# Seven of 22 gate and up tile pairs of a feed-forward block by Strassen's identity instead of five, with the input sums made earlier and laid partly into the weight slots

## The chip, the cores and the metric

One core of one Trainium2 chip runs the kernel. The metric is the device time of one execution in microseconds (us). The kernel before takes 2000.92 us (median of three runs, 2000.67 to 2001.42).

## What is computed

The reference is a model of two layers on 512 tokens of width 1024 with 16 meta tokens in front, so 528 token columns. A layer is a feed-forward block, a mixer (a gated linear recurrence beside a latent attention) and a second feed-forward block. All is float32. The change touches the feed-forward blocks alone:

```python
D_MODEL = 1024
D_FF = 11 * D_MODEL // 4

def swiglu(u, w_gate, w_up, w_down):
    return (jax.nn.silu(u @ w_gate) * (u @ w_up)) @ w_down

for l in range(DEPTH):
    f = swiglu(rms_norm(h, ffn1_pre_g[l]), ffn1_w_gate[l], ffn1_w_up[l], ffn1_w_down[l])
    h = h + 0.5 * rms_norm(f, ffn1_post_g[l])
    ...
    h = h + rms_norm(y, mix_post_g[l])
    f = swiglu(rms_norm(h, ffn2_pre_g[l]), ffn2_w_gate[l], ffn2_w_up[l], ffn2_w_down[l])
    h = h + 0.5 * rms_norm(f, ffn2_post_g[l])
return h[:, N_META:]
```

## The kernel before, in words

**Layout and precision.** Features lie on the 128 partitions, tokens along the free dimension. The tokens are split into two halves of 264 columns. The last feed-forward block needs only the 512 real tokens, so its halves have 256 columns. A float32 product is made of three matmuls: high part of the weights by high part of the input, high by low, low by high. The input's parts are `xh` and `xl`, the weights' are `whi` and `wlo`.

**Blocks.** Six blocks run one after another (b = 0 to 5); blocks 0, 2, 3 and 5 are feed-forward blocks, 1 and 4 are mixers. A feed-forward block has 22 pairs of a gate tile and an up tile (m = 0 to 21), each tile with 8 chunks of 128 input features, and then the down product from `hidh` and `hidl`, the two parts of the hidden values. The first three tiles are interleaved in `opening` (L1871), because their input arrives half by half; all later ones go through `product` (L1821) or `strassen` (L1833).

**Weight slots.** Every weight tile takes the next of four slots in turn. SyncE loads it into `raw` (`load`, L663), ScalarE rounds it into `whi` (`hi`, L789), and GpSimd subtracts the two into `wlo` in four pieces (`lo`, L741) or VectorE does in one (`low`, L1464). TensorE waits for that low part at the head of each tile (`slot_in`, L1815). A slot has 11 x 128 columns, since a down tile needs them; a gate or up tile uses 8 x 128. Tile numbers count from the block's first: in a plain pair m they are 2m and 2m + 1 as long as no Strassen pair came before.

**Strassen pairs.** A pair m in `STRASSEN` (L119: 5, 7, 9, 11, 13) does gate and up together as a 2 x 2 block product with seven half products instead of eight: rows are the gate's and the up's weights, the inner split is between the upper and the lower four feature chunks, columns are the two token halves. Such a pair takes four slots, of the kinds gate, s13, s2up and s4. The kinds s13 and s4 are sums of weights that VectorE makes in `raw` (`sums`, L1439), and VectorE makes their low parts too. The seven half products are 12 matmuls of half a token row each:

```python
part(n[1], False, sums(0), bank(uu, trim, 1))
pe.wait_ge(part_copied, q + 1)
part(n[1], True, sums(2), bank(z, trim, 0)).then_inc(slots_used, 1)
```

The first half product stands in PSUM until ScalarE copies it out (`part_copy`, L992), and the fourth half product reuses its bank, which is the wait in the middle line. VectorE joins the seven results in `strassen_sums` (L1471).

**Input sums.** The sums of input chunks are the same for every Strassen pair of a block and are made once, in four steps k = 0 to 3. Step k: ScalarE writes the scaled chunks k and k + 4 into `t_in` (`sum_inputs`, L977); VectorE makes four sums of them in `t_sum`, each of half a token row (`t_sums`, L1420, the instructions of L1428 to L1431); ScalarE rounds them into `t_hi` (`sum_hi`, L987); VectorE subtracts into `t_lo` (`t_low`, L1433). There is one `t_in` and one `t_sum`, so a step's sums wait for the step before. TensorE waits for all four steps once per block, before its first s13 tile.

**Order.** Each engine works through a list written out by hand. ScalarE's loop over m (L1001) is: silu, the rounding of the tiles 2m + 4 and 2m + 5, and the rounding of the hidden values (`hid_hi`, L974), with the parts of the input sums between them. VectorE's loop (L1500) is: gate out of PSUM (L1395), up out of PSUM (L1403), their product `hid` (L1411), its low part (`hid_lo`, L1416), and between them `sums`, `low`, `t_low` and `t_sums`. The silu waits for gate, hid for silu, hid_hi for hid, and hid_lo for hid_hi, so ScalarE and VectorE wait for each other twice in every pair. TensorE has four pairs of PSUM banks in turn; before the last chunk of a tile it waits until the next tile's banks have been read (`unit_free`, L1818).

Of the kernel before, what the change touches and what calls it, by code (L numbers as in the profile page):

```python
# [25 lines left out]
F32 = mybir.dt.float32  # L26
F32R = mybir.dt.float32r
BF16 = mybir.dt.bfloat16
ALU = mybir.AluOpType
ACT = mybir.ActivationFunctionType  # L30
AX = mybir.AxisListType

P = 128
# [4 lines left out]
T = N_META + SEQ  # L38
HALF = T // 2
D = 1024  # L40
DC = D // P
# [12 lines left out]
RING = 4  # L54
# [61 lines left out]
DVE_TAIL = (0, 2, 4, 6, 7)  # L116


STRASSEN = (5, 7, 9, 11, 13)  # L119
KH = DC // 2  # L120
T_SUMS = 4


def build_program(nc, a, out, depth, d_ff):
    FC = d_ff // P
    FH = FC // 2
    MAXT = max(FH, DC)
# [1 line left out]
    assert FC % 2 == 0 and FC >= 6  # L129


    assert FC - DC > max(STRASSEN) and FC - DC - 4 > min(STRASSEN) > 4


    tiles = []
# [2 lines left out]
    for b in range(NB):  # L138
# [4 lines left out]
        for m in range(FC):  # L143
            n = len(tiles)
# [17 lines left out]
    for n in range(NSLOT):  # L162
        made[n in LO_DVE] += 1
        LO_N[n] = made[n in LO_DVE]
        if KIND.get(n) not in ("s13", "s4"):
# [5 lines left out]
                     k=4, q=HEADS, statl=1, v=len(V_UNITS), tr=WC, out=DC)  # L171
    U = {}
    n = 0
# [10 lines left out]
    for b in range(NB):  # L184
        if b % 3 != 1:
            n = U[b, "gu"]
# [100 lines left out]
    with ExitStack() as ctx:  # L287
# [4 lines left out]
        base = [(nc.sbuf_base + 31) // 32 * 32]  # L292

        def sb_at(name, offset, shape, dt):
            return nc.alloc_sbuf_tensor_at(name, shape, dt, offset=offset)

        def sb(name, shape, dt):
            size = 2 if dt == BF16 else 4
            for s in shape[1:]:
                size *= s  # L300
            t = sb_at(name, base[0], shape, dt)
            base[0] += (size + 31) // 32 * 32
            return t

        CH = T * 4
# [4 lines left out]
        xl = sb("xl", [P, DC, T], F32R)  # L310
        tail_step = sb_at("tail_step", xh_at, [P, DC, T], F32)
        f_ffn = sb_at("f_ffn", xl_at, [P, DC, T], F32)
        raw = sb("raw", [P, RING, MAXT * P], F32)
        whi = sb("whi", [P, RING, MAXT * P], F32R)
        wlo = sb("wlo", [P, RING, MAXT * P], F32R)
# [10 lines left out]
        arena = base[0]  # L326
# [1 line left out]
        hidh = sb_at("hidh", arena, [P, FC, T], F32R)  # L328
        hidl = sb_at("hidl", arena + FC * CH, [P, FC, T], F32R)

        t_hi = sb_at("t_hi", arena + (FC - DC) * CH, [P, KH, T_SUMS, HALF], F32R)
        t_lo = sb_at("t_lo", arena + (2 * FC - DC) * CH, [P, KH, T_SUMS, HALF], F32R)
        t_in = sb_at("t_in", arena + (FC - DC - 4) * CH, [P, 2, T], F32)
        t_sum = sb_at("t_sum", arena + (FC - DC - 2) * CH, [P, T_SUMS, HALF], F32)

        off = [arena]

# [162 lines left out]
        t_hi_ready = sem("t_hi_ready")  # L500
# [279 lines left out]
        def _(act):  # L780
# [8 lines left out]
            def hi(n):  # L789
                if n < NSLOT:  # L790
                    r, k = n % RING, tiles[n] * P

                    if n in PREV:
                        act.wait_ge(slots_used, slot_used(PREV[n]))
                    if KIND.get(n) in ("s13", "s2up", "s4"):
                        act.wait_ge(w_sums, 3 * STRASSEN_N[n] + ("s13", "s2up", "s4").index(KIND[n]) + 1)
                    else:
                        act.wait_ge(raw_full[r], 16 * LOADED_N[n])
                    nc.scalar.activation(w_hi(n)[:, 0:k], raw[:, r, 0:k], ACT.Copy).then_inc(hi_ready, 1)  # L799
# [160 lines left out]
            def ffn(b):  # L960
                s0, f0 = slot0[b], (b // 3 * 2 + b % 3 // 2) * FC
                u0, trim = U[b, "gu"], b > 0 and trimmed(b - 1)

                F = b // 3 * 2 + b % 3 // 2
                g = ("ffn1_pre_g", "mix_pre_g", "ffn2_pre_g")[b % 3]

                def silu(m):
                    ug = GATE_U[b, m]
                    act.wait_ge(psum_free[pair_of(ug)], read_out(ug))
                    nc.scalar.activation(toks(tmp[2], trim), toks(tmp[0], trim), ACT.Silu).then_inc(silu_ready, 1)  # L970

                def hid_hi(m):
                    act.wait_ge(hid_ready, f0 + m + 1)
                    nc.scalar.activation(toks(hidh[:, m, :], trim), toks(tmp[3], trim),  # L974
                                         ACT.Copy).then_inc(hidh_ready, 1)

                def sum_inputs(k):  # L977

                    if k:
                        act.wait_ge(t_sum_ready, KH * F + k)  # L980
                    for i in range(2):
                        c = k + i * KH
                        ins = nc.scalar.activation(toks(t_in[:, i, :], trim), toks(h[:, c, :], trim), ACT.Copy,
                                                   scale=col(g, b // 3, c))
                    ins.then_inc(t_in_ready, 1)

                def sum_hi(k):  # L987
                    act.wait_ge(t_sum_ready, KH * F + k + 1)
                    nt = span(trim, 0)[1]
                    nc.scalar.activation(t_hi[:, k, :, 0:nt], t_sum[:, :, 0:nt], ACT.Copy).then_inc(t_hi_ready, 1)  # L990

                def part_copy(m):  # L992

                    q = STRASSEN_N[TILES_OF[b, m][0]]
                    act.wait_ge(part_mm, 2 * q + 1)
                    if q:
                        act.wait_ge(part_added, 6 * q)
                    nc.scalar.activation(half(tmp[4], trim, 0), bank(FIRST_U[b, m], trim, 0), ACT.Copy)\
                        .then_inc(part_copied, 1)

                for m in range(FC):  # L1001
                    n = TILES_OF[b, m]
                    if m in STRASSEN:
                        part_copy(m)
                        for i in range(3):
                            hi(n[i] + RING)
                        silu(m)
                        hi(n[3] + RING)
                        hid_hi(m)
                        continue  # L1010
                    silu(m)
                    if m:
                        hi(n[0] + RING)
                    if m == 1:
                        sum_hi(0)
                        sum_inputs(1)
                    hid_hi(m)
                    hi(n[1] + RING)
                    if 0 < m < 4:
                        sum_hi(m)  # L1020
                    if m < 3 and m != 1:
                        sum_inputs(0 if m == 0 else 3)
                    elif m == 1:
                        sum_inputs(2)
                tables(LN_EXP_TABLES)
                for m in range(DC - split[b]):
                    hi(out_slot(b, m) - 1 + RING)
                    output_chunk(b, m)
                    hi(out_slot(b, m) + RING)
# [194 lines left out]
        def _(dve):  # L1224
# [158 lines left out]
            def ffn(b):  # L1383
# [36 lines left out]
                def t_sums(k):  # L1420
# [9 lines left out]
                    chain.link(nc.vector.tensor_tensor(t2, b22, t1, ALU.subtract))  # L1430
                    nc.vector.tensor_tensor(t4, b21, t2, ALU.subtract).then_inc(t_sum_ready, 1)  # L1431

                def t_low(k):  # L1433
                    dve.wait_ge(t_hi_ready, KH * F + k + 1)
                    nt = span(trim, 0)[1]
                    nc.vector.tensor_tensor(t_lo[:, k, :, 0:nt], t_sum[:, :, 0:nt],
                                            t_hi[:, k, :, 0:nt].bitcast(F32), ALU.subtract).then_inc(t_lo_ready, 1)

                def sums(n):  # L1439

# [60 lines left out]
                for m in range(FC):  # L1501
                    n = TILES_OF[b, m]
                    nxt = [i + RING for i in n]
                    sums(nxt[0])
                    if m in STRASSEN:
                        strassen_sums(m, 0)
                        sums(nxt[1])
                        low(nxt[0])
                        sums(nxt[2])
                        low(nxt[1])  # L1510
                        strassen_sums(m, 1)
                        strassen_sums(m, 2)
                        low(nxt[2])
                        strassen_sums(m, 3)
                        gate(m)
                        up(m)
                        sums(nxt[3])
                        hid(m)
                        low(nxt[3])
                        hid_lo(m)  # L1520
                        continue
                    gate(m)
                    if m == 1:
                        t_sums(0)
                    elif 2 <= m <= 4:
                        t_low(m - 1)
                    sums(nxt[1])
                    low(nxt[0])
                    up(m)
                    hid(m)  # L1530
                    low(nxt[1])
                    hid_lo(m)
                    if m == 1:
                        t_low(0)
                    if 1 <= m <= 3:
                        t_sums(m)
                    if b == 0 and m == FC - 4:
                        decay_rates()
                output_sum(b)
# [251 lines left out]
        def _(pe):  # L1791
# [41 lines left out]
            def strassen(b, m, trim, following):  # L1833
# [18 lines left out]
                    return lambda k: (xh[:, k + upper * KH, at:at + nt], xl[:, k + upper * KH, at:at + nt])  # L1852

                def sums(i):
                    return lambda k: (t_hi[:, k, i, 0:nt], t_lo[:, k, i, 0:nt])

                slot_in(n[0])
                part(n[0], False, tokens(0, a0), bank(z, trim, 0), ug).then_inc(part_mm, 1)
# [473 lines left out]
```

## Time and profile before

| | |
|---|---|
| median of three runs | 2000.92 us (2000.67 to 2001.42) |
| the profiled execution | 2001.3 us, of which the span from first to last instruction is 1999.5 us |
| TensorE matmul busy | 1986.0 us, 99% of the span, 15084 instructions |
| VectorE, ScalarE, GpSimd busy | 913.9, 824.6, 1029.3 us |
| DMA | 175.76 MB, mean 88 GB/s |
| mean granted clock | 0.999 |

Busy times overlap one another. A busy TensorE says nothing of how well it is fed; what matters is where its stream of matmuls breaks. A matmul's own duration is longer than its share of the stream, since they are pipelined, so lengths of work on TensorE are read as differences of start times.

### The profile page before, as it was taken

The numbers are of one execution on the slowest core, as the hardware profiler recorded it, in microseconds if no ns is written. First come the engines' busy times: TensorE is split into PE (matmuls) and PEld (weight loads), VectorE is DVE, ScalarE is ACT, GpSimd is POOL, SyncE is SP. The second block draws the span as 40 slices with busy tenths as digits, with TensorE's granted clock in tenths as the row PEclk, the third lists the DMA queues.
The fourth block names the chain that finished last, engine by engine and source line by source line (L and its number), as shares of the span: only waits on it lengthen the run. The fifth ranks groups of instructions, "written<-read, shape, count | busy, mean of one in ns | idle before, by whom it ended". The sixth has DMA issues, their size and how long they took to land.

```text
span 1999.5 us, 35699 instructions
## 1 busy us (share of the span) xinstructions
PE 1986.0 (99%) x15084; PEld 1909.5 (96%) x15084; DVE 913.9 (46%) x1433; ACT 824.6 (41%) x1318; POOL 1029.3 (51%) x1257
## 2 busy tenths in 40 slices
PE   9999999999999999999999999999999999999998
PEld 9999999999899999999999999999998998888887
DVE  6663310478546765210076542103785467642102
ACT  6433222465555533232264332224555465332321
POOL 3655554576315655454375554544763256564551
PEclk9999999999999999999999999999999999999999
DMA  4224332132201223332122333321322112333321
GB/s 167 86 94 125 103 102 86 67 96 80 64 33 43 85 85 127 100 117 88 57 75 85 96 117 111 102 84 62 101 82 65 33 54 74 109 124 107 116 73 43
DMA packets 48479, 175.76 MB, mean 88 GB/s; under 512 B 5184, under 2 KB 9408, under 8 KB 48320
## 3 DMA queue, kind: packets, MB, share of 16 engines
q1 hardware_dynamic: 48176, 173.40, 26.6%
q8 instruction: 118, 1.93, 0.4%
q14 instruction: 41, 0.34, 0.1%
q10 hardware_dynamic: 144, 0.10, 0.0%
HBM read 171.38 MB, written 2.10 MB: 87 GB/s over the span
## 4 chain that ended last, share of the span: by engine, by line
PE 98%; DVE 1%; ACT 1%; DMA 0%; issue 0%; SPq 0%; DVEq 0%
PE ps L1803 97%; PE ps L2184 1%; DMA h<-in_x 0%; DVE osb L1751 0%; ACT xh L829 0%; DVE xl L1761 0%; DVE tail_step L1295 0%; PE ps L2063 0%; DVE probT L1719 0%; ACT prob L1151 0%; DVE small L1728 0%; DVE h L1300 0%; ACT tmp L1187 0%; ACT xh L1202 0%; DVE wlo L1329 0%
## 5 line engine op out<-in xcount | busy, mean ns | idle before, releaser
L747 POOL TENSOR_TENSOR wlo<-raw,whi 128x256 fp32r<-128x256 f32 (+2 forms) x1148 | 944.0, 854 | 726.2 <-ACT whi L799 723.6
L1803 PE MATMUL ps<-xh,whi 128*128 128x264 f32 (+2 forms) x2680 | 645.3, 296 | 3.2 <-DVE xl L1334 1.5
L1803 PE MATMUL ps<-xl,whi 128*128 128x264 f32 (+2 forms) x2680 | 641.7, 295 | 0.0
L1803 PE MATMUL ps<-xh,wlo 128*128 128x264 f32 (+2 forms) x2680 | 640.8, 295 | 0.0
L1803 PEld LDWEIGHTS ps<-xh,whi 128*128 128x128 f32 x2680 | 445.0, 188 | 17.4 <-DVE wlo L1329 2.3
L799 ACT ACTIVATE whi<-raw 128x1024 fp32r<-128x1024 f32 (+3 forms) x329 | 356.0, 1083 | 255.7 <-PE ps L1803 221.6
L1803 PEld LDWEIGHTS ps<-xl,whi 128*128 128x128 f32 x2680 | 443.7, 188 | 11.4
L1803 PEld LDWEIGHTS ps<-xh,wlo 128*128 128x128 f32 x2680 | 443.6, 189 | 10.5
L1803 PE MATMUL ps<-hidh,whi 128*128 128x264 f32 (+2 forms) x1276 | 313.6, 296 | 0.0
L1803 PE MATMUL ps<-hidl,whi 128*128 128x264 f32 (+2 forms) x1276 | 312.5, 295 | 0.0
L1803 PE MATMUL ps<-hidh,wlo 128*128 128x264 f32 (+2 forms) x1276 | 312.4, 295 | 0.0
L1373 DVE TENSOR_TENSOR tmp<-tmp,tmp 128x264 f32<-128x264 f32 (+3 forms) x52 | 36.2, 696 | 414.5 <-ACT tmp L862 361.1
L1803 PEld LDWEIGHTS ps<-hidl,whi 128*128 128x128 f32 x1276 | 214.4, 188 | 6.2
L1803 PEld LDWEIGHTS ps<-hidh,wlo 128*128 128x128 f32 x1276 | 214.0, 188 | 5.9
L1803 PEld LDWEIGHTS ps<-hidh,whi 128*128 128x128 f32 x1276 | 213.3, 188 | 6.0
L1403 DVE TENSOR_TENSOR tmp<-ps,rs_in 128x528 f32<-128x528 f32 (+1 forms) x88 | 61.6, 700 | 211.7 <-PE ps L1803 211.7
L974 ACT ACTIVATE hidh<-tmp 128x528 fp32r<-128x528 f32 (+1 forms) x88 | 56.2, 639 | 233.3 <-DVE tmp L1411 233.3
L970 ACT ACTIVATE tmp<-tmp 128x528 f32<-128x528 f32 (+1 forms) x88 | 56.4, 641 | 182.9 <-DVE tmp L1395 182.4
L1395 DVE TENSOR_TENSOR tmp<-ps,rs_in 128x528 f32<-128x528 f32 (+1 forms) x88 | 61.7, 701 | 98.0 <-PE ps L1803 82.3
L763 POOL TENSOR_TENSOR tmp<-tmp,tmp 128x264 f32<-128x264 f32 (+1 forms) x55 | 45.7, 830 | 103.3 <-ACT tmp L836 100.5
L1803 PE MATMUL ps<-t_lo,whi 128*128 128x264 f32 (+1 forms) x320 | 90.5, 283 | 0.0
L1803 PE MATMUL ps<-t_hi,whi 128*128 128x264 f32 (+1 forms) x320 | 90.5, 283 | 0.0
(218 smaller groups left out, 2332.8 us busy)
## 6 DMA issues: line engine op xcount, KB each, us to landing
raw<-in_ffn_up SPq DMA_DIRECT2D x88, 512.0 KB, 3.7
raw<-in_ffn_down SPq DMA_DIRECT2D x64, 704.0 KB, 4.0
raw<-in_ffn_gate SPq DMA_DIRECT2D x87, 512.0 KB, 3.6
raw<-in_w_in SPq DMA_DIRECT2D x28, 512.0 KB, 3.5
raw<-in_w_out SPq DMA_DIRECT2D x16, 512.0 KB, 3.6
raw<-in_w_q SPq DMA_DIRECT2D x8, 384.0 KB, 3.2
out_t<-h SPq DMA_DIRECT2D x16, 128.0 KB, 1.8
h<-in_x SPq DMA_DIRECT2D x2, 528.0 KB, 5.7
```

What stands on the lines that cost most here:

```text
L747: ins = nc.gpsimd.tensor_tensor(w_lo(n)[:, at], raw[:, r, at], w_hi(n)[:, at].bitcast(F32), ALU.subtract)
L763: nc.gpsimd.tensor_tensor(hs, hs, square_of(k, s, trim), ALU.add)\
L799: nc.scalar.activation(w_hi(n)[:, 0:k], raw[:, r, 0:k], ACT.Copy).then_inc(hi_ready, 1)
L970: nc.scalar.activation(toks(tmp[2], trim), toks(tmp[0], trim), ACT.Silu).then_inc(silu_ready, 1)
L974: nc.scalar.activation(toks(hidh[:, m, :], trim), toks(tmp[3], trim), ACT.Copy).then_inc(hidh_ready, 1)
L1373: nc.vector.tensor_tensor(acc, acc, part(tmp[m % 2], trim), ALU.add).then_inc(sum_ready, 1)
L1395: nc.vector.tensor_tensor(halves(tmp[0], trim), unit(ug, trim, trim and m > 1 and m not in STRASSEN), halves(rs_in, trim), ALU.mult).then_ ...
L1403: nc.vector.tensor_tensor(halves(tmp[1], trim), unit(uu, trim, trim and m > 0 and m not in STRASSEN), halves(rs_in, trim), ALU.mult).then_ ...
L1803: return nc.tensor.matmul(o, w, x, start=start, stop=stop)
L2184: ins = nc.tensor.transpose(ps[:, c0:c0 + P], prob[e % 4][:, k0:k0 + P], ident)
```

## The change

The pairs that use the identity become 4, 6, 8, 10, 12, 14 and 16. The four steps of input sums no longer have a place of their own behind the hidden values: step 0's parts lie in columns 1024 to 1287 of the slots of `whi` and `wlo`, step 1's high part in the same columns of `raw` and its low part in the last hidden chunk, steps 2 and 3 in hidden chunks 17 to 20. The steps are placed earlier in both engines' lists: ScalarE copies step 0's input ahead of the first silu, and VectorE makes step 0's sums at the end of pair 0, step 1's and 2's in pair 1, step 3's at the end of pair 2.

```diff
-STRASSEN = (5, 7, 9, 11, 13)
+STRASSEN = (4, 6, 8, 10, 12, 14, 16)
...
-        t_hi = sb_at("t_hi", arena + (FC - DC) * CH, [P, KH, T_SUMS, HALF], F32R)
-        t_lo = sb_at("t_lo", arena + (2 * FC - DC) * CH, [P, KH, T_SUMS, HALF], F32R)
-        t_in = sb_at("t_in", arena + (FC - DC - 4) * CH, [P, 2, T], F32)
-        t_sum = sb_at("t_sum", arena + (FC - DC - 2) * CH, [P, T_SUMS, HALF], F32)
+        hid_all = sb_at("hid_all", arena, [P, 2, FC, T], F32R)
+        raw_spare = sb_at("raw_spare", raw_at, [P, RING, MAXT * P], F32R)
+        spare = slice(DC * P, DC * P + HALF)
+
+        def four(first, which):
+            return hid_all[:, which, first:first + 2, :].rearrange("p a (i t) -> p (a i) t", i=2)
+
+        last = hid_all[:, :, FC - 1, :].rearrange("p a (i t) -> p a i t", i=2)
+        T_HI = [whi[:, :, spare], raw_spare[:, :, spare], four(FC - 5, 0), four(FC - 3, 0)]
+        T_LO = [wlo[:, :, spare], last, four(FC - 5, 1), four(FC - 3, 1)]
...
+        t_in = sb_at("t_in", arena + (FC - 9) * CH, [P, 2, T], F32)
+        t_sum = sb_at("t_sum", arena + (FC - 7) * CH, [P, T_SUMS, HALF], F32)
...
+                sum_inputs(0)
                 for m in range(FC):
...
                     if m == 1:
+                        sum_hi(1)
+                        sum_inputs(2)
+                    hid_hi(m)
+                    hi(n[1] + RING)
+                    if m == 0:
                         sum_hi(0)
                         sum_inputs(1)
-                    hid_hi(m)
-                    hi(n[1] + RING)
-                    if 0 < m < 4:
-                        sum_hi(m)
-                    if m < 3 and m != 1:
-                        sum_inputs(0 if m == 0 else 3)
                     elif m == 1:
-                        sum_inputs(2)
+                        sum_hi(2)
+                        sum_inputs(3)
+                    elif m == 2:
+                        sum_hi(3)
...
                     gate(m)
                     if m == 1:
-                        t_sums(0)
-                    elif 2 <= m <= 4:
-                        t_low(m - 1)
+                        t_low(0)
+                        t_sums(1)
+                    elif 2 <= m <= 3:
+                        t_low(m)
                     sums(nxt[1])
                     low(nxt[0])
                     up(m)
                     hid(m)
                     low(nxt[1])
                     hid_lo(m)
-                    if m == 1:
-                        t_low(0)
-                    if 1 <= m <= 3:
-                        t_sums(m)
+                    if m == 0:
+                        t_sums(0)
+                    elif m == 1:
+                        t_low(1)
+                        t_sums(2)
+                    elif m == 2:
+                        t_sums(3)
...
                 def sums(i):
-                    return lambda k: (t_hi[:, k, i, 0:nt], t_lo[:, k, i, 0:nt])
+                    return lambda k: (t_one(T_HI, k, i, nt), t_one(T_LO, k, i, nt))
```

## Rows read from the trace of the kernel before

**Rows 1.** The page's first part, busy time of each engine.
```profile
PE 1986.0 (99%) x15084; PEld 1909.5 (96%) x15084; DVE 913.9 (46%) x1433; ACT 824.6 (41%) x1318; POOL 1029.3 (51%) x1257
```

**Rows 2.** Waits of TensorE: who for whom, total, times, longest (us).
```profile
PE ps L1803 <- DVE xl L1334: 1.5, 2, 1.0
```

**Rows 3.** Timeline of TensorE, blocks 0 and 5: start, duration, instruction.
```profile
57.75 0.41 PE L1803 MATMUL ps<-xh,whi 128*128 128x264 f32 x2
...
69.49 0.28 PE L1803 MATMUL ps<-xh,whi 128*128 128x264 f32 x1
...
73.89 0.28 PE L1803 MATMUL ps<-t_hi,whi 128*128 128x264 f32 x1
...
79.71 0.40 PE L1803 MATMUL ps<-xh,whi 128*128 128x264 f32 x2
...
1672.11 0.40 PE L1803 MATMUL ps<-xh,whi 128*128 128x512 f32 x1
...
1683.23 0.28 PE L1803 MATMUL ps<-xh,whi 128*128 128x256 f32 x1
...
1687.48 0.28 PE L1803 MATMUL ps<-t_hi,whi 128*128 128x256 f32 x1
...
1693.10 0.39 PE L1803 MATMUL ps<-xh,whi 128*128 128x512 f32 x1
```

**Rows 4.** Timeline of ScalarE, the first pairs of block 0.
```profile
29.93 0.65 ACT L970 ACTIVATE tmp<-tmp 128x528 f32<-128x528 f32 x1
...
32.91 1.35 ACT L983 ACTIVATE t_in<-h,par 128x528 f32<-128x528 f32 x2
...
37.51 1.09 ACT L990 ACTIVATE t_hi<-t_sum 128x1056 fp32r<-128x1056 f32 x1 [1.76 <-DVE t_sum L1431]
```

**Rows 5.** Timeline of VectorE, the first five pairs of block 0.
```profile
32.09 0.71 DVE L1416 TENSOR_TENSOR hidl<-tmp,hidh 128x528 fp32r<-128x528 f32 x1 [0.71 <-ACT hidh L974]
...
34.30 0.52 DVE L1428 TENSOR_TENSOR t_sum<-t_in 128x264 f32<-128x264 f32 x1 [0.88 <-ACT t_in L983]
...
40.42 0.71 DVE L1416 TENSOR_TENSOR hidl<-tmp,hidh 128x528 fp32r<-128x528 f32 x1 [1.08 <-ACT hidh L974]
...
42.40 0.78 DVE L1428 TENSOR_TENSOR t_sum<-t_in 128x264 f32<-128x264 f32 x1
...
45.77 0.69 DVE L1395 TENSOR_TENSOR tmp<-ps,rs_in 128x528 f32<-128x528 f32 x1
47.00 1.26 DVE L1436 TENSOR_TENSOR t_lo<-t_sum,t_hi 128x1056 fp32r<-128x1056 f32 x1 [0.54 <-ACT t_hi L990]
...
59.47 1.21 DVE L1411 TENSOR_TENSOR tmp<-tmp,tmp 128x528 f32<-128x528 f32 x1
...
64.10 0.43 DVE L1428 TENSOR_TENSOR t_sum<-t_in 128x264 f32<-128x264 f32 x1
...
65.73 0.68 DVE L1455 TENSOR_TENSOR raw<-raw 128x512 f32<-128x512 f32 x1
66.33 0.70 DVE L1395 TENSOR_TENSOR tmp<-ps,rs_in 128x528 f32<-128x528 f32 x1
66.96 1.26 DVE L1436 TENSOR_TENSOR t_lo<-t_sum,t_hi 128x1056 fp32r<-128x1056 f32 x1
```

**Rows 6.** Timeline of GpSimd, block 0: two tiles' low parts.
```profile
33.09 6.86 POOL L747 TENSOR_TENSOR wlo<-raw,whi 128x256 fp32r<-128x256 f32 x8 [2.61 <-ACT whi L799]
```

**Rows 7.** The page's sixth part: loads of up tiles, KB each, us to landing.
```profile
raw<-in_ffn_up SPq DMA_DIRECT2D x88, 512.0 KB, 3.7
```

**Rows 8.** Timelines of VectorE and ScalarE, pair 4 of block 5.
```profile
1681.80 0.69 DVE L1395 TENSOR_TENSOR tmp<-ps,rs_in 128x512 f32<-128x512 f32 x1
...
1686.66 0.36 ACT L998 ACTIVATE tmp<-ps 128x256 f32<-128x256 f32 x1
```

**Rows 9.** Windows, end of the run: length, busy by engine, granted clock, DMA.
```profile
1992.00:1994.00 2.00, 0.00 (x0) 0.00 (x0) 1.31 (x4) 0.63 (x2) 0.48 (x1) 1.00 0.00 0
...
1996.00:1999.50 3.50, 0.00 (x0) 0.00 (x0) 1.11 (x4) 0.00 (x0) 0.36 (x1) 0.50 0.59 198
```

More of the change, by code:

```diff
@@ L129, in build_program @@
     assert FC % 2 == 0 and FC >= 6
-    assert FC - DC > max(STRASSEN) and FC - DC - 4 > min(STRASSEN) > 4
+    assert FC - 5 > max(STRASSEN) and FC - 9 > min(STRASSEN) > 3 and FH >= DC + 3
     tiles = []
@@ L312, in build_program @@
         f_ffn = sb_at("f_ffn", xl_at, [P, DC, T], F32)
+        raw_at = base[0]
         raw = sb("raw", [P, RING, MAXT * P], F32)
@@ L329, in build_program, with t_half, t_one, t_whole @@
         hidl = sb_at("hidl", arena + FC * CH, [P, FC, T], F32R)
-        t_hi = sb_at("t_hi", arena + (FC - DC) * CH, [P, KH, T_SUMS, HALF], F32R)
-        t_lo = sb_at("t_lo", arena + (2 * FC - DC) * CH, [P, KH, T_SUMS, HALF], F32R)
-        t_in = sb_at("t_in", arena + (FC - DC - 4) * CH, [P, 2, T], F32)
-        t_sum = sb_at("t_sum", arena + (FC - DC - 2) * CH, [P, T_SUMS, HALF], F32)
+        hid_all = sb_at("hid_all", arena, [P, 2, FC, T], F32R)
[6 more added lines that the diff above has]
+        T_LO = [wlo[:, :, spare], last, four(FC - 5, 1), four(FC - 3, 1)]
+        def t_half(part, k, nt):
+            at = part[k]
+            if at is last:
+                return at[:, :, :, 0:nt]
+            return at[:, :, 0:nt]
+        def t_one(part, k, i, nt):
+            at = part[k]
+            if at is last:
+                return at[:, i // 2, i % 2, 0:nt]
+            return at[:, i, 0:nt]
+        def t_whole(k, nt):
+            at = t_sum[:, :, 0:nt]
+            return at.rearrange("p (a i) t -> p a i t", i=2) if T_LO[k] is last else at
+        t_in = sb_at("t_in", arena + (FC - 9) * CH, [P, 2, T], F32)
+        t_sum = sb_at("t_sum", arena + (FC - 7) * CH, [P, T_SUMS, HALF], F32)
         off = [arena]
@@ L1431, in t_sums, with t_high @@
                     nc.vector.tensor_tensor(t4, b21, t2, ALU.subtract).then_inc(t_sum_ready, 1)
+                def t_high(k, nt):
+                    at = t_half(T_HI, k, nt).bitcast(F32)
+                    return at.rearrange("p (a i) t -> p a i t", i=2) if T_LO[k] is last else at
                 def t_low(k):
@@ L1435, in t_low @@
                     nt = span(trim, 0)[1]
-                    nc.vector.tensor_tensor(t_lo[:, k, :, 0:nt], t_sum[:, :, 0:nt],
-                                            t_hi[:, k, :, 0:nt].bitcast(F32), ALU.subtract).then_inc(t_lo_ready, 1)
+                    nc.vector.tensor_tensor(t_half(T_LO, k, nt), t_whole(k, nt), t_high(k, nt), ALU.subtract).then_inc(t_lo_ready, 1)
                 def sums(n):
```

2 lines of the change are left out of this document (1 added, 1 removed).

## Prediction, made before the changed kernel was run

> **What bounds the kernel now.** The page's busy times come first: TensorE's matmuls fill 1986.0 of 1999.5 us and no other engine is over 52% [rows 1]. Then the waits of TensorE: its longest kind of wait in the matmul line totals 1.5 us [rows 2]. So time is the number of matmuls times their spacing, as long as nothing starves the stream; an engine at half load costs nothing unless it is late at one place. The timeline of TensorE gives the spacing [rows 3]: plain pair 4 of block 0 runs from 57.75 to 69.49, 11.74 us for 96 matmuls of 264 columns, and Strassen pair 5 from 69.49 to 79.71, 10.22 us for 84. Both come to 0.122 us per matmul, so that weights used once instead of twice in a row cost nothing. In block 5 a plain pair (48 matmuls of 512 columns) takes 1683.23 - 1672.11 = 11.12 us and a Strassen pair (84 of 256) 1693.10 - 1683.23 = 9.87 us. The remaining question is whether the first Strassen pair, now pair 4, finds its operands in time; for that I read ScalarE, VectorE and GpSimd at the block's start.
>
> **The gain.** Each of the four blocks gets two more Strassen pairs. In blocks 0, 2 and 3: 6 x (11.74 - 10.22) = 9.1 us. In block 5: 2 x (11.12 - 9.87) = 2.5 us. Together 11.6 us, all on TensorE's path. The Trainium skill (TensorE: Matmul & The Clock Gate, "Wait — 56ns, not 53.3ns?") puts the spacing of back-to-back matmuls at N / 2.4 GHz plus about 2.5 ns, 112.5 ns for 264 columns; the trace has 122, and by the page six pairs would save 8.1 us instead of 9.1.
>
> **What the new pairs ask of the others.** A Strassen pair adds weight sums, PSUM sums and the low parts of s13 and s4 on VectorE, one rounding more on ScalarE, nothing on GpSimd (it makes two low parts per pair in both kinds) and no bytes (two loads either way). The Strassen and plain pairs alternate as before, and between pairs 5 and 14 TensorE shows no wait of weight [rows 2], so I cost pairs 6 to 16 at nothing beyond their matmuls. Their cover is the plain pair in between. The decay work of block 0 at m = 18 stays behind a plain pair.
>
> **The first Strassen pair comes 11.7 us sooner, its input sums do not.** TensorE starts the fourth half product of the pair, the one behind the part copy, 73.89 - 69.49 = 4.40 us after the pair's start [rows 3]. With pair 4 this place moves to 57.75 + 4.40 = 62.15 us in block 0. Against it stands a chain of ScalarE and VectorE that does not depend on TensorE, since all tiles it needs are long done. I follow it from rows of the old order, step by step; starts of consecutive instructions on one engine lie about 0.1 us closer than their durations.
>
> 1. ScalarE copies step 0's input ahead of silu(0): 1.35 us [rows 4], so silu(0) starts at 31.2 instead of 29.93. The low part of hidden chunk 0, at 32.09 before [rows 5], starts at 33.35, and VectorE is free for the first sums at 34.0.
> 2. Sums of step 0. Before, they took from 34.30 to the rounding at 37.51, 3.2 us [rows 4, 5], while GpSimd worked [rows 6]; the same sums with GpSimd idle take 65.73 - 64.10 = 1.6 us [rows 5]. The two slow each other. Tile 5's rounding is 1.3 us later too, so GpSimd runs from about 34.3 to 37.8 (6.86 us for two tiles [rows 6]): I take the slow price, and the rounding starts at 37.2.
> 3. Rounding of step 0 and input of step 1 (1.09 and 1.35 us [rows 4]): 39.6.
> 4. Sums of step 1. GpSimd's next tile waits for silu(1) and a rounding behind that input, about 41.1, so the fast price holds: 41.3.
> 5. Rounding of step 1, input of step 2, rounding of hidden chunk 1. The old distance from a rounding at 37.51 to the low part at 40.42 held the same three: 2.9 us [rows 4, 5], giving 44.25. Then the low parts of chunk 1 and of step 1, as from 40.42 to 42.40, 2.0 us: 46.25.
> 6. Sums of step 2 with GpSimd on tile 7: 42.40 to 45.77, 3.4 us [rows 5]; gate(2) starts at 49.6. Low part of step 2 done 47.00 + 1.26 - 45.77 = 2.5 us later: 52.1.
> 7. Two s13 weight sums at 0.68 us [rows 5] and up(2), 0.6: hid(2) starts at 54.0. The load of tile 10 that they need is issued when tile 6's low part is done, about 44.5, and lands after 3.7 us [rows 7], 4 us ahead.
> 8. From hid(2) over the rounding and low part of s13 to the sums of step 3: 64.10 - 59.47 = 4.6 us [rows 5], 58.65. From there to gate(3): 66.33 - 64.10 = 2.2 us, 60.9.
> 9. From gate(3) to the end of t_low(3): 66.96 + 1.26 - 66.33 = 1.9 us, 62.8. From gate(3) to the end of the part copy, which stands in ScalarE's list behind silu(3), tile 10, hid_hi(3) and tile 11: 1686.66 + 0.36 - 1681.80 = 5.2 us where up did not wait [rows 8], plus up to 0.5 us if hid(3) meets GpSimd (1.21 us, against 0.71 for a low part of the same size [rows 5]): 66.4.
>
> So TensorE, which wants the third half product at 62.15 - 12 x 0.122 = 60.7, waits about 2.1 us for the last low part, then computes 1.5 us, then waits about 2.1 us for the part copy: 4.25 us in all. In the kernel before the same t_low was done at 68.2 against a need at 72.4: four us of slack, and the chain has gained only 5.4 us (gate at 66.33 before, 60.9 now) where TensorE's need has moved by 11.74.
>
> In block 5 the old gate(4) started 1687.48 - 1681.80 = 5.7 us ahead of the fourth half product [rows 3, 8], in block 0 73.89 - 66.33 = 7.6 us. Moving need by 11.12 and gate by 5.4 leaves no lead at all, so the wait is the 5.45 us of step 9. Blocks 2 and 3 I take like block 0, having the same forms. Sum: 3 x 4.25 + 5.45 = 18.2 us of waits. What is queued behind: VectorE and ScalarE don't wait on TensorE here, but SyncE's loads of tiles 12 and 13 wait for the last weight sum of pair 4; they land before TensorE is through with the delayed pair.
>
> The new places of the sums (spare columns of slots, other hidden chunks) have the same sizes and partitions; I cost them at nothing, from below and above by at most 2% of a 1.26 us subtraction.
>
> **Sum.** -11.6 + 18.2 = +6.6 us. The profiled execution took 2001.3 us, 0.4 above the median, so it would be 2007.9, and the median 2007.5.
>
> **Bounds.** What the rows don't settle is whether GpSimd is in its pieces at each sum. Down: step 0's sums at the fast price, -1.6, both hid products fast, -0.75: a wait of 1.9 in the first three and 3.1 in block 5 leaves 1998.1. Up: step 1's sums slow as well, +1.7, and hid(3) slow, +0.25: 6.2 and 7.4 us, 2015.3. I take middle values as the order of starts says; not all ends come at once.
>
> **Rivals.**
> *The chain arrives in time.* If it were under 2.9 us late on average (11.6 / 4), the change gains. That needs 1.4 us less than my steps in every block, for instance step 0's sums ahead of GpSimd. For it: the wide gap between the two prices, and that the slow one depends on a few tenths. Against: steps 3, 5, 8 and 9 are plain latencies between two engines that repeat within 0.1 us. With no wait at all the time is 1989.3; with half of it, 1998.4.
> *More contention.* A later tile 5 on GpSimd overlaps step 1's sums and passes the delay on: up to 7 us more, 2014.
> *The clock falls during the waits.* Granted clock stayed at 1.00 (2.4 GHz) in a 2 us window without a single matmul and showed 0.50 (1.2 GHz) only in the last window, over 5 us after the last matmul [rows 9]. My waits are two pieces near 2 us with 12 matmuls in between, so I expect no fall. If the remaining 48 matmuls of pair 4 ran at the lower level, each block would lose 48 x 0.122 = 5.9 us, 2031. The Trainium skill (TensorE: Matmul & The Clock Gate, "What's actually happening") says that the throttled state is the default and activity releases it; by that rule a fall is possible, and the rows speak against it here.
> *The change doesn't shorten the pairs*, because matmuls reading sums beside weights in one slot are slower: the gain is gone, the wait stays, 2019. No row shows such a conflict.
>
> **How the numbers follow.** About 0.2%, 4 us, is what a measurement of this kernel can tell from no change. Forecast, with waits of 3.1 to 6.2 us per block on average, 2001 to 2014: 0.78; of it 0.10 lies under 2004.9, where the waits average under 3.9 us against my 4.55. In time or half so, clearly faster: 0.10. Between the two, 1997 to 2001: 0.03. Contention beyond the range 0.04, the clock 0.03, no saving 0.02, all slower. So faster 0.10, same 0.10 + 0.03 = 0.13, slower 0.68 + 0.09 = 0.77. The range is the forecast's own, 2001 to 2014; it holds the bounds above but for the corner where every doubt falls one way, and leaves out the in-time case, the clock and the lost saving.
>
> **What would show it.** Right: in each feed-forward block the waits of TensorE name t_lo (or gate(3)'s read) and the part copy, some 4 to 5.5 us together; pairs of 10.2 and 11.7 us alternate from pair 6 on; gate(3) at 60.9 and the part copy ending at 66.4 in block 0; granted clock 1.00. Wrong: no wait in pair 4 (then time near 1989), waits in pair 6 or later, or a matmul spacing off 0.122 us.

## The result and the profile after

The changed kernel takes 2012.12 us (median of five runs, 2010.93 to 2012.76) against 2000.8 us before (median of five runs), a ratio of 1.0056 with a 95% interval of 1.0041 to 1.0070: 11.3 us slower. The forecast was 2007.5 us, slower, in a range of 2001 to 2014. The profiled execution is the slowest of the five, so what is read from its trace adds up to 0.6 us more than the median.

| | before | after |
|---|---|---|
| profiled execution, span | 2001.3 us, 1999.5 us | 2012.76 us, 2011.0 us |
| matmul busy | 1986.0 us | 1982.4 us |
| mean granted clock | 0.999 | 0.994 |

The waits of TensorE come first (who for whom, total, times, longest; the matmul helper is now L1840). Before, the longest kind of wait in this line totalled 1.5 us [rows 2]:

```profile
PE ps L1840 <- ACT tmp L1025: 6.8, 4, 2.2
PE ps L1840 <- DVE tmp L1425: 5.4, 4, 1.7
PE ps L1840 <- DVE hid_all L1470: 2.4, 4, 0.7
...
PE ps L1840 <- POOL wlo L774: 0.4, 1, 0.4
```

Three waits occur four times, once per feed-forward block: for the part copy (L1025), for the read of gate(3) (L1425), and for the last low part of the input sums (L1470). The forecast named all three, the first two of them as one piece. The timeline of TensorE shows them inside pair 4 of block 0:

```profile
57.49 0.29 PE L1840 MATMUL ps<-xh,whi 128*128 128x264 f32 x1
...
61.45 0.40 PE L1840 MATMUL ps<-xh,whi 128*128 128x264 f32 x1 [1.25 <-DVE tmp L1425]
...
62.73 0.36 PE L1840 MATMUL ps<-whi 128*128 128x264 f32 x1 [0.63 <-DVE hid_all L1470]
...
64.02 0.64 PE L1840 MATMUL ps<-hid_all,whi 128*128 128x264 f32 x2
64.46 0.42 PE L1840 MATMUL ps<-hid_all,wlo 128*128 128x264 f32 x1
66.61 0.59 PE L1840 MATMUL ps<-whi 128*128 128x264 f32 x1 [1.73 <-ACT tmp L1025]
...
74.29 0.41 PE L1840 MATMUL ps<-xh,whi 128*128 128x264 f32 x2
```

The pair runs from 57.49 to 74.29, 16.8 us instead of the 10.2 of an undisturbed one. And a matmul of 264 columns at 66.61 has a duration of 0.59 us, where the same form has 0.28 elsewhere: the clock. Windows of 3 us over that stretch (length; busy of TensorE, its weight loads, VectorE, ScalarE, GpSimd; granted clock; DMA):

```profile
60.00:63.00 3.00, 1.11 (x7) 0.73 (x6) 3.00 (x5) 2.66 (x3) 0.00 (x0) 1.00 0.00 0
63.00:66.00 3.00, 1.88 (x12) 1.57 (x10) 2.05 (x3) 0.90 (x3) 2.90 (x4) 0.62 0.58 164
66.00:69.00 3.00, 2.38 (x11) 2.39 (x12) 1.66 (x3) 1.62 (x3) 1.09 (x3) 0.50 0.93 343
69.00:72.00 3.00, 3.00 (x21) 3.00 (x21) 0.34 (x1) 1.06 (x1) 3.00 (x5) 0.74 0.07 23
```

After a window with 7 matmuls the granted clock falls to 0.50, the lower level of 1.2 GHz, and comes back inside the window from 69 to 72. It fell before the wait for the part copy began: from 64.02 to 64.46 two matmuls start 0.22 us apart instead of 0.12, and that wait begins only behind them. In blocks 3 and 5, where the clock fell too, it was the same. The next two windows lie there, ahead of the wait for the part copy; the two waits before it were 1.23 and 0.65 us in block 3, 1.73 and 0.51 in block 5:

```profile
1070.70:1071.40 0.70, 0.70 (x5) 0.61 (x3) 0.70 (x1) 0.00 (x0) 0.70 (x2) 0.50 0.30 70
...
1685.10:1686.00 0.90, 0.39 (x3) 0.12 (x2) 0.90 (x2) 0.90 (x2) 0.00 (x0) 0.50 0.00 0
```

In block 2 the same waits left it at 1.00:

```profile
684.00:687.00 3.00, 1.50 (x10) 1.33 (x11) 3.00 (x5) 2.28 (x3) 0.51 (x1) 1.00 0.00 0
687.00:690.00 3.00, 0.82 (x7) 0.61 (x6) 1.74 (x3) 1.44 (x3) 2.76 (x4) 1.00 0.76 231
```

The chain of VectorE and ScalarE, by the rows of the same instructions as in the forecast:

```profile
49.53 0.69 DVE L1425 TENSOR_TENSOR tmp<-ps,rs_in 128x528 f32<-128x528 f32 x1
...
53.88 0.97 DVE L1441 TENSOR_TENSOR tmp<-tmp,tmp 128x528 f32<-128x528 f32 x1
...
58.47 0.42 DVE L1458 TENSOR_TENSOR t_sum<-t_in 128x264 f32<-128x264 f32 x1
...
60.69 0.70 DVE L1425 TENSOR_TENSOR tmp<-ps,rs_in 128x528 f32<-128x528 f32 x1
61.32 1.26 DVE L1470 TENSOR_TENSOR hid_all<-t_sum,hid_all 128x1056 fp32r<-128x1056 f32 x1
```

```profile
36.95 1.09 ACT L1017 ACTIVATE whi<-t_sum 128x1056 fp32r<-128x1056 f32 x1 [2.92 <-DVE t_sum L1461]
...
66.19 0.37 ACT L1025 ACTIVATE tmp<-ps 128x264 f32<-128x264 f32 x1
```

Rounding of step 0 at 36.95 (forecast 37.2), gate(2) at 49.53 (49.6), hid(2) at 53.88 (54.0), the sums of step 3 at 58.47 (58.65), gate(3) at 60.69 (60.9), t_low(3) done at 62.6 (62.8), the part copy done at 66.56 (66.4). The whole block begins 0.24 us earlier in this execution. With that taken off, gate(3) and t_low(3) came as worked out within 0.05 us, and the part copy 0.4 us later: the steps from gate(3) to its end were that much longer.

**Where the 11.6 us went.** From the last matmul of one pair to the last of the next, in the changed kernel pair 4 takes 16.80, 15.06, 16.83 and 16.06 us in blocks 0, 2, 3 and 5, where undisturbed Strassen pairs of the same trace take 10.19 and, in block 5, 10.06. That is 24.1 us too much. With pair 4 counted at its undisturbed length, all pairs together are 12.5 us shorter than before. In every pair from 5 on there is no wait. 24.1 - 12.5 = 11.6 us, which is the whole difference of the two spans within 0.1.

### The profile page after: what moved, and what is told of

Read it like the earlier page. It is cut to its first block, busy times and chain, and to the rows that moved or that the text cites. A ratio compares the mean times of both kernels' runs of the same rounds, so it can differ in the third digit from the quotient of the medians.

```text
span 2011.0 us, 35915 instructions
## 1 busy us (share of the span) xinstructions
PE 1982.4 (99%) x15084; PEld 1906.8 (95%) x15084; DVE 967.1 (48%) x1537; ACT 841.4 (42%) x1342; POOL 1023.8 (51%) x1257
## 4 chain that ended last, share of the span: by engine, by line
PE 90%; DVE 5%; ACT 3%; issue 1%; DMA 0%; DVEq 0%; SPq 0%; ACTq 0%
PE ps L1840 89%; PE ps L2221 1%; DVE tmp L1441 1%; DVE t_sum L1459 1%; DVE t_sum L1461 1%; DVE t_sum L1460 0%; ACT t_in L1010 0%; DVE t_sum L1458 0%; ACT whi L826 0%; DVE hidl L1446 0%; DVE tmp L1433 0%; ACT hidh L1001 0%; ACT L813 0%; DVE wlo L1470 0%; DMA h<-in_x 0%
## 5 line engine op out<-in xcount | busy, mean ns | idle before, releaser
L1840 PE MATMUL ps<-xh,whi 128*128 128x264 f32 (+2 forms) x2552 | 621.1, 296 | 9.0 <-DVE tmp L1425 5.4
L1840 PE MATMUL ps<-xl,whi 128*128 128x264 f32 (+2 forms) x2552 | 616.0, 294 | 0.0
L1840 PE MATMUL ps<-xh,wlo 128*128 128x264 f32 (+2 forms) x2552 | 615.6, 294 | 0.0
L826 ACT ACTIVATE whi<-raw 128x1024 fp32r<-128x1024 f32 (+3 forms) x345 | 369.8, 1073 | 298.8 <-PE ps L1840 250.4
L1840 PEld LDWEIGHTS ps<-xh,whi 128*128 128x128 f32 x2552 | 426.7, 188 | 22.9 <-DVE tmp L1425 6.3
L1840 PEld LDWEIGHTS ps<-xl,whi 128*128 128x128 f32 x2552 | 425.5, 188 | 10.0
L1840 PEld LDWEIGHTS ps<-xh,wlo 128*128 128x128 f32 x2552 | 425.3, 188 | 9.1
L1840 PE MATMUL ps<-hidh,whi 128*128 128x264 f32 (+2 forms) x1276 | 313.5, 296 | 0.0
L1840 PE MATMUL ps<-hidl,whi 128*128 128x264 f32 (+2 forms) x1276 | 312.3, 295 | 0.0
L1840 PE MATMUL ps<-hidh,wlo 128*128 128x264 f32 (+2 forms) x1276 | 312.2, 295 | 0.0
L1840 PEld LDWEIGHTS ps<-hidl,whi 128*128 128x128 f32 x1276 | 214.2, 188 | 6.2
L1840 PEld LDWEIGHTS ps<-hidh,wlo 128*128 128x128 f32 x1276 | 213.8, 188 | 5.9
L1840 PEld LDWEIGHTS ps<-hidh,whi 128*128 128x128 f32 x1276 | 213.1, 188 | 6.0
L1840 PE MATMUL ps<-hid_all,whi 128*128 128x264 f32 (+1 forms) x560 | 116.0, 288 | 0.0
L1840 PEld LDWEIGHTS ps<-hid_all,whi 128*128 128x128 f32 x560 | 93.0, 194 | 0.0
L1425 DVE TENSOR_TENSOR tmp<-ps,rs_in 128x528 f32<-128x528 f32 (+1 forms) x88 | 61.6, 700 | 62.8 <-PE ps L1840 46.8
```

The lines of the kernel that those rows point to most:

```text
L1425: nc.vector.tensor_tensor(halves(tmp[0], trim), unit(ug, trim, trim and m > 1 and m not in STRASSEN), halves(rs_in, trim), ALU.mult).then_ ...
L1840: return nc.tensor.matmul(o, w, x, start=start, stop=stop)
```

## Experiments

Two theories stood for the size. A: the waits of pair 4, which the forecast has, plus a loss from the clock, to which it had given a chance of 0.03. Against it: slow operands in shared slots, or a load of seven pairs that is too high for VectorE wherever the first one stands. Each ratio below is to runs of the kernel before taken beside the experiment, whose medians lie from 2001.03 to 2001.29 us.

### The clock, by keeping TensorE at work in its waits

```diff
+                def fill(count):
+                    if m == STRASSEN[0]:
+                        for _ in range(count):
+                            mm(bank(z, trim, 1), xh[:, 1, a0:a0 + P], xh[:, 0, a0:a0 + nt], True, True)
...
+                            fill(filled)
...
-                part(n[0], True, tokens(1, a0), bank(ug, trim, 0), uu).then_inc(slots_used, 1)
+                part(n[0], True, tokens(1, a0), bank(ug, trim, 0), uu, 10).then_inc(slots_used, 1)
                 slot_in(n[1])
+                fill(6)
...
+                fill(16)
                 pe.wait_ge(part_copied, q + 1)
```

> The changed kernel with 32 matmuls of no use put into TensorE's three waits of pair 4 (10 ahead of the read of gate(3), 6 ahead of the last low part of the input sums, 16 ahead of the part copy; 32 x 0.122 = 3.9 us against waits of 4.2 us in block 0). They write a PSUM bank that the fifth half product overwrites. Theory A (waits of 17.6 us in all plus 6.6 us from a granted clock that falls during them): the clock stays at 1.00, pair 4 of block 0 takes 14.5 to 15 us instead of 16.8, the time falls by 4 to 7 us to 2005 to 2008. Rival B (the slow matmuls of pair 4 come from operands that share a slot with weights being written): the matmuls stay at 0.21 us, the time stays at 2012 or more. Rival C (waits are all of it, the clock costs nothing since TensorE waits for the same events anyway): the time stays within 1 us of 2012.

Measured: 2008.68 us (2008.58 to 2008.78), ratio to before 1.0038 (1.0024 to 1.0052). It is faster than the changed kernel by 3.4 us although it does 128 matmuls more. Theory A holds in kind but had the clock too dear: it expected 4 to 7 us less. Windows and timeline of this kernel over the same stretch:

```profile
60.00:63.00 3.00, 2.98 (x24) 2.72 (x23) 3.00 (x5) 2.68 (x3) 0.09 (x1) 1.00 0.00 0
63.00:66.00 3.00, 3.00 (x26) 2.92 (x24) 1.87 (x3) 1.06 (x2) 3.00 (x4) 1.00 0.64 193
66.00:69.00 3.00, 2.69 (x23) 2.56 (x22) 1.66 (x3) 1.91 (x4) 0.80 (x2) 1.00 0.90 328
```

```profile
57.31 0.29 PE L1840 MATMUL ps<-xh,whi 128*128 128x264 f32 x1
...
66.44 0.39 PE L1840 MATMUL ps<-whi 128*128 128x264 f32 x1 [0.31 <-ACT tmp L1025]
...
72.39 0.41 PE L1840 MATMUL ps<-xh,whi 128*128 128x264 f32 x2
```

The clock stays at 1.00. The fourth half product starts at 66.44, as late as before, behind a rest of 0.31 us of the same wait; after it the pair ends in 5.95 us instead of 7.68. Pair 4 takes 15.08 us in blocks 0, 2 and 3 and 15.45 in block 5. Block 2 of the changed kernel, whose clock stayed at 1.00 with the waits empty, takes 15.06: where the clock holds, filling changes nothing. That gives the split: three times 4.89 and once 5.39, so 20.1 us, are waits for the chain, and the 4.1 us that the pairs 4 of the changed kernel's trace take beyond that are the clock (3.4 between the medians). That the matmuls that read the sums run at full pace here, in the same places, tells against slow operands; rival C, a clock that costs nothing, falls too.

Then the same with only some of the waits filled (10 and 6, or 16 alone):

> As e1_fill, but with matmuls of no use only in the first two waits (10 and 6), the wait for the part copy left empty. In the changed kernel the clock fell inside pair 4; filling all three waits gave back 3.4 us. Theory A (it takes the empty waits together, and one empty wait of 2 us after full work is too little): the clock stays, 2008.7 within 1 us. Rival (the last, longest wait is what drops it): 2011 to 2012.5.

Measured: 2011.07 us (2010.23 to 2011.96), ratio 1.0050 (1.0033 to 1.0067).

> As e1_fill, but with 16 matmuls of no use only in the wait for the part copy; the first two waits (1.4 and 0.8 us in block 0) stay empty. Theory A (the first two alone are too little as well): the clock stays, 2008.7 within 1 us. Rival (they are what drops it): 2010 to 2012, and as the useless matmuls then run at half rate they may end after the part copy and add to it.

Measured: 2011.3 us (2009.71 to 2011.39), ratio 1.0047 (1.0030 to 1.0064).

Both theories A fall: with either share of the waits left empty most of the clock's cost is there again (2.4 and 2.6 us over the kernel with all of them filled), but not in every block. In the first of the two, pair 4 takes 15.07, 15.04, 16.58 and 15.48 us; in the second 15.03, 15.02, 16.02 and 16.88. Windows of the first in block 3, where the last wait was empty:

```profile
1067.00:1070.00 3.00, 2.40 (x20) 2.15 (x18) 2.96 (x4) 1.07 (x2) 1.86 (x3) 1.00 0.25 53
1070.00:1073.00 3.00, 1.34 (x9) 1.34 (x10) 1.77 (x4) 2.40 (x4) 1.40 (x2) 0.91 0.92 324
1073.00:1076.00 3.00, 3.00 (x16) 3.00 (x16) 0.02 (x1) 1.16 (x2) 2.83 (x5) 0.52 0.38 150
```

and of the second in block 0, where the first two were empty and the clock held:

```profile
60.00:63.00 3.00, 1.13 (x8) 0.73 (x7) 3.00 (x5) 2.48 (x3) 0.00 (x0) 1.00 0.00 0
63.00:66.00 3.00, 3.00 (x25) 3.00 (x26) 2.24 (x3) 0.89 (x3) 2.72 (x4) 1.00 0.53 139
```

The same gaps drop the clock in one block and not in another. The five runs of the changed kernel lie between 2010.93 us at a mean clock of 0.997 and 2012.76 at 0.994, where the kernel with all waits filled spreads by 0.2 us.

### The part copy alone

```diff
                     if m in STRASSEN:
-                        part_copy(m)
+                        if m > STRASSEN[0]:
+                            part_copy(m)
...
+                    if m == STRASSEN[0] - 1:
+                        part_copy(m + 1)
                     silu(m)
```

> The changed kernel with the part copy of the first Strassen pair ahead of silu(3) in ScalarE's list (pair 4 of each block only). Theory A: the copy ends near 62 us in block 0 instead of 66.6, so the third wait (2.0 us) goes, but the low part of tile 10 (66.4, now 0.3 us later) is late next, at the fifth half product, which would start at 65.7: a new wait near 1.1 us on GpSimd. Waits fall by 0.9 us per block, 3.6 us, and what the clock cost (6.6 us) goes partly, since the pieces are shorter: 2002 to 2008. Rival (the chain behind gate(3) is one and moves with it): no change, 2012.

Measured: 2006.2 us (2005.66 to 2007.14), ratio 1.0027 (1.0017 to 1.0037): 5.9 us off the changed kernel. Timelines of ScalarE, TensorE and GpSimd, block 0:

```profile
61.07 0.37 ACT L1025 ACTIVATE tmp<-ps 128x264 f32<-128x264 f32 x1
```

```profile
61.32 0.39 PE L1843 MATMUL ps<-xh,whi 128*128 128x264 f32 x1 [1.22 <-DVE tmp L1428]
...
62.60 0.36 PE L1843 MATMUL ps<-whi 128*128 128x264 f32 x1 [0.65 <-DVE hid_all L1473]
...
66.33 0.39 PE L1843 MATMUL ps<-whi 128*128 128x264 f32 x1 [0.58 <-POOL wlo L774]
```

```profile
62.99 3.28 POOL L774 TENSOR_TENSOR wlo<-raw,whi 128x256 fp32r<-128x256 f32 x4 [6.27 <-ACT whi L826]
```

The copy ends at 61.4, the two earlier waits stay, and what is late next is what was named: the low part of tile 10, done at 66.27. The pair takes 13.40 us with the clock at 1.00 in all its windows. The clock fell in block 2, whose pair takes 14.10, and in block 5, whose pair takes 15.09. The pairs 5 take 2.1 us too much together; at the head of that of block 5 TensorE waits 0.67 us for GpSimd once more.

### Where the first pair stands, and how many there are

```diff
-STRASSEN = (4, 6, 8, 10, 12, 14, 16)
+STRASSEN = (4, 6, 8, 10, 12)
```

> The changed kernel with five pairs at 4, 6, 8, 10, 12. Theory A (the loss belongs to the first pair at 4, whatever their number): in pair 4 the same 16 us as in the changed kernel, so the changed kernel's time plus the gain of two pairs, 2012.1 + 11.6 = 2023.7, within 2 us. Rival (the load of seven pairs has a part in it): 2015 to 2021.

Measured: 2023.21 us (2022.15 to 2024.22), ratio 1.0112 (1.0097 to 1.0128). Its waits:

```profile
PE ps L1840 <- ACT tmp L1025: 7.6, 4, 2.2
PE ps L1840 <- DVE tmp L1425: 5.5, 4, 1.7
PE ps L1840 <- DVE hid_all L1470: 2.6, 4, 0.7
```

The same three, as large as with seven pairs, and pair 4 at 15.06 to 16.60 us. The loss belongs to a first pair at 4, not to the number.

```diff
-STRASSEN = (4, 6, 8, 10, 12, 14, 16)
+STRASSEN = (5, 7, 9, 11, 13, 15, 16)
```

> The changed kernel with the seven Strassen pairs at 5, 7, 9, 11, 13, 15 and 16 instead of 4, 6, ... 16: new places, new order, the same number, the first one a pair later. Theory A: the chain of input sums and part copy ends near 66.6 us, TensorE needs it at 73.6 in block 0: no wait in the first Strassen pair, clock 1.00, and the whole gain of the shorter pairs stays: 2000.8 - 11.6 = 1989.2, if pair 16 right behind 15 is fed in time (VectorE has about 8 us of work for a Strassen pair of 10.2 us); up to 2 us per block more if it is not. Rival (seven pairs load VectorE too much whatever the first one is): over 2000.

Measured: 2001.86 us (2001.21 to 2002.5), ratio 1.0004 (0.9994 to 1.0013). The expectation missed by 12.7 us, by 4.7 even with the 2 us per block that it allowed for pair 16, and this kernel alone would have spoken for the rival. Its waits have other names:

```profile
PE ps L1840 <- POOL wlo L774: 4.0, 8, 1.2
PE ps L1840 <- ACT tmp L1025: 3.3, 5, 0.9
```

By pair: 16 and 17 take 8.6 us too much over the four blocks (11.25, 11.50, 11.25, 12.15 and 12.06, 12.44, 12.24, 12.46 us), pairs 4 and 5 of the four blocks some 4 us. In block 2 TensorE waits 0.91 us for the part copy inside pair 16 and 0.45 us for GpSimd's low part at the head of pair 17. Two causes, then. The runs below take them apart.

### The order and the places of the input sums

The old five pairs (5, 7, 9, 11, 13), first in the changed kernel as it is:

> The changed kernel with the old five pairs (5, 7, 9, 11, 13): the new places and the new order of the input sums alone. Theory A: no wait in pair 5 and the same matmuls, so the time before, 2000.8 within 0.5. Rival (the new places slow the matmuls that read them, or the earlier order delays something): over 2002.

Measured: 2003.78 us (2003.54 to 2004.0), ratio 1.0013 (1.0004 to 1.0023). The rival held: the moves cost 2.7 us though nothing else changed. Then the same five pairs with the new places and the old order of both lists:

```diff
-                sum_inputs(0)
                 for m in range(FC):
...
                     if m == 1:
-                        sum_hi(1)
-                        sum_inputs(2)
+                        sum_hi(0)
+                        sum_inputs(1)
                     hid_hi(m)
                     hi(n[1] + RING)
-                    if m == 0:
-                        sum_hi(0)
-                        sum_inputs(1)
+                    if 0 < m < 4:
+                        sum_hi(m)
+                    if m < 3 and m != 1:
+                        sum_inputs(0 if m == 0 else 3)
                     elif m == 1:
-                        sum_hi(2)
-                        sum_inputs(3)
-                    elif m == 2:
-                        sum_hi(3)
+                        sum_inputs(2)
```

(VectorE's list goes back in the same way.)

> The new places of the input sums with the old order of both engines' lists and the old five pairs (5, 7, 9, 11, 13). Theory A (the 2.8 us that the same five pairs cost with the new order come from the order alone, since VectorE now does three steps of sums ahead of gate(2), 49.7 instead of 45.8, and every weight tile after it is late by as much): the time before, 2000.8 to 2001.3. Rival (they come from the places): 2003 to 2004.

Measured: 2000.54 us (2000.06 to 2000.8), ratio 0.9997 (0.9988 to 1.0006): the places are free, the order has the cost. Timelines of the first of the two kernels, VectorE's gate(2), ScalarE's rounding of step 2's sums and of tile 8, TensorE's waits in blocks 0 and 5:

```profile
49.68 0.69 DVE L1425 TENSOR_TENSOR tmp<-ps,rs_in 128x528 f32<-128x528 f32 x1
```

```profile
49.78 1.09 ACT L1017 ACTIVATE hid_all<-t_sum 128x1056 fp32r<-128x1056 f32 x1 [4.62 <-DVE t_sum L1461]
...
52.56 1.05 ACT L826 ACTIVATE whi<-raw 128x1024 fp32r<-128x1024 f32 x1
```

```profile
75.55 0.39 PE L1840 MATMUL ps<-whi 128*128 128x264 f32 x1 [0.17 <-POOL wlo L774]
...
1673.11 0.50 PE L1840 MATMUL ps<-xh,whi 128*128 128x512 f32 x1 [0.77 <-POOL wlo L774]
```

and gate(2) and the rounding of tile 8 with the old order:

```profile
45.40 0.69 DVE L1422 TENSOR_TENSOR tmp<-ps,rs_in 128x528 f32<-128x528 f32 x1
```

```profile
48.29 1.05 ACT L826 ACTIVATE whi<-raw 128x1024 fp32r<-128x1024 f32 x1
```

VectorE makes three steps of sums instead of two ahead of gate(2). ScalarE waits 4.62 us for the third of them, because the rounding of step 2 and the input of step 3 stand ahead of silu(2) in its list, and silu(2) and the rounding of tile 8 stand behind them. Both gate(2) and the rounding of tile 8 come 4.3 us later than with the old order, and the tiles after it are later too. In block 5, where TensorE is quickest, tile 8's low part is late by itself.

### Seven pairs that begin at 5 and stand apart

The bound on the last pair was one pair tighter than needed: hidden chunk 17, in which step 2's sums begin, is written only after pair 17 has read them.

```diff
-    assert FC - 5 > max(STRASSEN)
+    assert FC - 5 >= max(STRASSEN)
-STRASSEN = (4, 6, 8, 10, 12, 14, 16)
+STRASSEN = (5, 7, 9, 11, 13, 15, 17)
```

With the old order:

> The new places, the old order, and seven pairs that begin at 5 and stand apart: 5, 7, 9, 11, 13, 15, 17. Theory A: no wait in any pair, the whole gain of two shorter pairs in four blocks: 2001.0 - 11.6 = 1989.4, within 1 us. Rival (seven pairs a block are too much for VectorE and GpSimd, as the 2001.9 of the seven with 15 and 16 side by side may be read): 1995 or more, with waits for GpSimd's low parts behind pair 15.

Measured: 1988.85 us (1988.7 to 1988.97), ratio to before 0.9939 (0.9926 to 0.9953), 12.2 us faster than the kernel before and 23.3 faster than the changed one. Its longest waits are the two at the start of the run, as before:

```profile
PE ps L1830 <- DVE maskb L1253: 1.7, 1, 1.7
PE ps L1833 <- DVE wlo L1356: 0.9, 1, 0.9
```

and pair 5 of block 0 runs from one first matmul to the next in 10.19 us:

```profile
69.09 0.29 PE L1833 MATMUL ps<-xh,whi 128*128 128x264 f32 x1
...
79.28 0.41 PE L1833 MATMUL ps<-xh,whi 128*128 128x264 f32 x2
```

With the new order:

> As the seven at 5 to 17, with the new order. Theory A: the order's own 2.8 us and nothing else: 1992.2 within 1 us; then the rest of what 5, 7, ... 15, 16 lost (8.4 us of waits in pairs 16 and 17) is the price of two Strassen pairs side by side. Rival: the same as the old order, 1989.4.

Measured: 1992.92 us (1992.66 to 1992.99), ratio 0.9959 (0.9946 to 0.9973): 4.1 us more than with the old order, somewhat more than the 2.7 to 3.2 that the order cost five pairs; pair 5 of block 3 is one place, 11.30 us here and 10.61 with five pairs, for which no run gives the reason. The difference to the seven with 15 and 16 side by side is 8.9 us, which agrees with the 8.6 us read from its pairs: that is the price of two Strassen pairs without a plain one between them.

## Why the prediction was right, and what it missed

**Right: the sign and the mechanism.** The gain of 11.6 us is there: 12.2 in the seven pairs at 5 to 17, 12.5 in the pairs of the changed kernel. Against it stand the three waits in pair 4, one each per block, with the names given; gate(3)'s read, given as the other name of the first piece, is a wait of its own. All seven times of the chain named above came within 0.3 us. The choice that carried it was step 2 and step 6 at the price under GpSimd and step 4 at the price without: VectorE's four sums took 3.2 and 3.4 us in steps 0 and 2, and 1.64 us in step 1. The in-time rival was excluded by that: it needed 1.65 us less per block on the forecast's own average (4.55 - 2.9; the 1.4 in its text fits blocks 0, 2 and 3 alone). The lower end of the range, 2001, likewise belongs to waits of 2.9 us per block, not 3.1; neither slip changes the result.

**Mis-sized: the waits, 20.1 us for 18.2.** By the kernel with filled waits they are 4.89 us in blocks 0, 2 and 3 for 4.25, and 5.39 in block 5 for 5.45. Of the 0.64 us that each of the first three is over, 0.4 is step 9, from gate(3) to the end of the part copy: 5.87 us for 5.5. In it hid(3) met GpSimd and took 1.25 us, about 0.2 more than was taken for it. The rest is mostly the start-up of the matmul stream after a wait, which the sum did not have: behind the last wait the filled pair needs 5.95 us, where an undisturbed one needs 5.8. In block 5 the low part of tile 8 was late as well, at the pair's head, which the forecast had not looked at. Its 0.6 us are part of the 5.39, since the chain ends later in any case; that the total is so near 5.45 is partly luck.

**Missed: the clock, 4.1 us.** The step that failed is the sentence "My waits are two pieces near 2 us with 12 matmuls in between, so I expect no fall". The row behind it [rows 9] showed a clock that holds through 2 us without a matmul after full work. It did not show a second gap close behind the first, and the granted clock fell in three of four blocks of the profiled execution, each time after the first two waits or in the second (1.25 and 0.63 us in block 0) and before the third. The window with 0.50 in that row begins 4.3 us after the last matmul ends, at 1991.73, and not over 5:

```profile
1990.40 1.33 PE L1803 MATMUL ps<-tmp,consts 128*128 128x256 f32 x4
```

The rival had the mechanism but a price, 5.9 us per block, for a fall that lasts to the pair's end; the falls cost 1.7, 1.7 and 0.6 us, since part of each lay inside the wait and the clock was back before the pair was over. That the time stayed inside the range is luck as far as these 4.1 us go: the range left the clock out, and its upper part stood for contention that did not come. The Trainium skill's rule (TensorE: Matmul & The Clock Gate, "What's actually happening"), that the throttled state is the default and activity releases it, fits the result; I had let one row speak against it. By the Trainium skill (TensorE: Matmul & The Clock Gate, "Wait — 56ns, not 53.3ns?") the spacing of back-to-back matmuls of 264 columns would be 112.5 ns; 10.19 us for 84 of them in pair 5 is 121 ns, and the measurement decides.

**Costed at nothing, and not free: the earlier order.** The forecast priced the moved steps only by when the sums come. It did not ask what the moved work pushes back: 2.7 us with five pairs, 4.1 with seven. In the changed kernel no pair behind 4 shows it; that the larger waits of pair 4 cover it is argued, not shown. The earlier places in the lists brought gate(3) forward by 5.4 us (66.33 to 60.69, less the 0.24 us of the block's earlier start), where the first pair's need moved by 11.7.

**Right by cover: pairs 6 to 16 at nothing.** The cover named was the plain pair in between, and with it taken away (15 and 16 side by side) it costs some 2.2 us per block.

What stays open: why the clock falls in one block and not in another. In the changed kernel every fall came ahead of the wait for the part copy; the two half-filled kernels show that either share can drop it, in some blocks.

## What to carry to other kernels

When a cheaper form of work is to start earlier, write down how much earlier its first user needs its operands and how much earlier the chain that makes them gets; if the second is smaller, start one step later and extend the list at its end instead: here that, with the old order of the sums kept, turned 11.3 us of loss into 12.2 us of gain (8.1 with the new order). Work moved forward in an in-order list pushes back what stands behind it, here gate(2) by 4.3 us, so price both. And count a wait of a few microseconds in the matmul stream at more than its length, because the clock can fall with it.

## What the runs showed of the hardware that was not expected

- The granted clock fell to its lower level (windows at 0.62, 0.50 and 0.74) around gaps of at most 2.2 us without a matmul, with matmuls between them, and the same gaps left it at 1.00 in another block of the same execution. At the lower level the matmuls of 264 columns in the rows above start 0.22 us apart (two of them from 64.02 to 64.46) instead of 0.12.
- The new places made the undisturbed pairs slightly shorter in blocks 0, 2 and 3: 10.19 and 11.72 us instead of 10.22 and 11.76 with the same matmuls (five pairs, old order). In block 5 the Strassen pairs became longer, 10.06 us instead of 9.98. The time differs by 0.5 us and its ratio of 0.9997 does not set it apart from no change; why the lengths change was not tried.
